# First adaLN scale of a two-layer decoder trunk: a quarter of three column groups computed on GpSimd

## The chip, the cores and the metric

One core of one Trainium2 chip runs the whole program. The metric is the device time of one execution in microseconds (us). The kernel before took 2666.12 us (median of 3 runs, 2662.95 to 2666.7).

## The reference, cut to what matters

Two decoder layers on 256 tokens of 2048 numbers, all in float32. The part that the change touches is the very first modulation of layer 0, before the first matrix product:

```python
cond = jax.nn.silu(c)                                   # c: 1 x 2048
mod = (cond @ ada_w[0] + ada_b[0])[:, None, :]          # ada_w[0]: 2048 x 12288
sh1, sc1, g1, sh2, sc2, g2 = jnp.split(mod, 6, axis=-1)
h = rmsnorm(x, norm_mix[0]) * (1.0 + sc1) + sh1         # sh1 the shift, sc1 the scale
y = nsa_mla_mixer(h, positions, rel_bias, even_w_in[0], ...)   # begins with h @ w_in
```

So `sc1` is a vector of 2048 numbers, each a sum over 2048 rows of `ada_w`, and `h @ w_in` can't begin on a piece of `h` before that piece of `sc1` and `sh1` is known.

## The kernel before, in words

**Prologue.** The first stage works in four column groups g = 0 to 3 of 512 columns. For each group SyncE (SP) loads four units of 512 rows x 512 columns (1 MB) of the scale's weights into the ring `RAW` (4 slots of 1 MB), four such units of the shift's weights into a ring of its own, `PRO`, and, in between, units of `even_w_in` for three column chunks c0, c1, c2 of the first projection into `RAW` as well. The order of the ring is fixed by `make_plan`: scale(g,0), c2's unit of group g-1, scale(g,1), scale(g,2), c0's unit g, c1's unit g, scale(g,3). SP waits in program order: before it loads unit s it waits until whoever reads unit s-4 has finished with that slot (`load` in `sync_program`).

**Scale, before.** `scale_rows(g, i)` on TensorE (PE) multiplies each 128-row piece of the unit by the matching column of `COND` (128 x 1): four float32 matmuls of 1 x 512, which the trace records as 8, collected in PSUM bank 6 over all 16 row pieces. ScalarE (ACT) copies the 1 x 512 row to `ROW` (`row_kept`, line 740). `columns(g)` turns it into columns: 4 matmuls with `ROW` as stationary operand and one element of ones (line 1279), and 4 with `ACC` (line 1283), where VectorE (DVE) has built the shift's partial products by `shift(g, i)` (lines 1832 and 1835).

**After `columns(g)`.** `opened(g)` on DVE (lines 1894, 1895, 1897) makes shift and gain, then for each of four row blocks DVE writes `TF` (line 1887), ACT writes the high part `AHI` (line 745), and DVE the low part `ALO` (line 1820). `opening_unit(c0, g)` on PE (lines 1199 to 1201) begins with the first of these `ALO` blocks; it is 24 matmuls of 128 x 512. On PE the order of a group is: `scale_rows(g,0)`, `opening_unit(c0, g-1)`, a bias piece (48 small matmuls, line 1238), `scale_rows(g,1)`, `opening_unit(c1, g-1)`, `scale_rows(g,2)`, a bias piece, `opening_unit(c2, g-1)`, `scale_rows(g,3)`, `columns(g)`. Thus `scale_rows(g,0)` stands between `columns(g-1)` and the opening unit that needs its result. After `columns(3)` no scale rows are left, and PE goes on to the last opening units with nothing in between.

**The other engines there.** For each weight unit ACT writes the high part `WHI` (line 622) and DVE the low part `WLO` (line 1722). GpSimd (POOL) does nothing in the prologue: it waits for `bias_kept`, to issue the load of a bias row (line 594).

After the prologue the same ring `RAW` feeds every product of the kernel, and PE works through all of them in order.

Of the kernel before, what the change touches and what calls it, by code (L numbers as in the profile page):

```python
# [20 lines left out]
ALU, ACT, AX = mybir.AluOpType, mybir.ActivationFunctionType, mybir.AxisListType  # L21

P, T, D, FF = 128, 256, 2048, 5632
KT = D // P
EPS, NEG = 1e-6, -1e30
RING = 4
SH1, SC1, G1, SH2, SC2, G2 = range(6)
# [3 lines left out]
ADA_ORDER = [((layer, seg), kt) for layer, seg, a, b in (  # L31
    (0, G1, 0, 16), (0, SC2, 0, 16), (0, SH2, 0, 16), (0, G2, 0, 16),
    (1, SH1, 0, 8), (1, SC1, 0, 16), (1, SH1, 8, 16), (1, SC2, 0, 16), (1, G1, 0, 16), (1, SH2, 0, 16), (1, G2, 0, 16))
    for kt in range(a, b)]
ADA_DONE = {vec: n + 1 for n, (vec, kt) in enumerate(ADA_ORDER) if kt == KT - 1}
ADA_APART = (1, SH1)
# [92 lines left out]
class Plan:  # L129

    def __init__(self):
        self.s = self.w = self.a = self.r = 0
        self.last = [None, None, None]
        self.kinds = []

    def unit(self, kind, **kw):
        u = Unit(kind, self.s, {"w": self.w, "a": self.a, "r": self.r}[kind], self.w, self.a, self.r, **kw)
        self.s += 1
        self.w += kind == "w"
        self.a += kind == "a"  # L140
        self.r += kind == "r"
        self.kinds.append(kind)
        return u

# [44 lines left out]
class Machine:  # L189

    def __init__(self, nc, t, ctx, known):
# [3 lines left out]
        def sb(name, shape, dt=F32):  # L195
            return ctx.enter_context(nc.sbuf_tensor(name, shape, dt))

        def overlay(*groups):

            size, made = 0, []  # L200
            for group in groups:
                with ExitStack() as one:
# [11 lines left out]
        ((self.AHI, self.ALO), (_, self.XG), (self.O, self.KN, self.RP, self.KRO, self.HCT, self.KCT, self.VCN), (_, self.BF)) = overlay(  # L214
            [("AHI", [P, KT, T], F32R), ("ALO", [P, KT, T], F32R)],
            [("XG_ROOM", [P, KT, T], F32), ("XG", [P, KT, T], F32)],
            [("O", [P, 16, T], F32), ("KN", [P, 8, T], F32), ("RP", [P, 2, 8, 64], F32), ("KRO", [P, 2, P], F32),
# [3 lines left out]
        (self.GHI, self.GLO), (self.PRO,), (self.XT, self.CQH, self.CQL), (_, self.QN), (self.KT_F, self.V_F) = overlay(  # L221
            [("GHI", [P, KT, T], F32R), ("GLO", [P, KT, T], F32R)],
            [("PRO", [P, RING, 2048], F32)],
# [17 lines left out]
        self.VC = sb("VC", [P, V_ALL])  # L241
        self.COND = sb("COND", [P, KT])
        self.GS = sb("GS", [P, 4, KT])
        self.SHM = sb("SHM", [P, 4, KT])
# [30 lines left out]
        self.W2C = self.S2[:, 1, :].rearrange("p (i k n) -> p i k n", i=2, k=2)  # L275
        self.RR = self.S2[:].rearrange("p a b -> p (a b)").rearrange("p (b h n) -> p b h n", b=2, h=8)
        self.PTC = (self.PT[:].rearrange("p a b c -> p (a b c)")[0:15, 0:1024], self.L[:].rearrange("p a b c -> p (a b c)")[0:15, 512:1536])
        self.OH = [s[:].rearrange("p a b -> p (a b)").bitcast(BF16)[:, 0:2048].rearrange("p (i t) -> p i t", t=P)
                   for s in (self.ST, self.S2)]

# [52 lines left out]
    def make_plan(self, t):  # L333
        plan = self.plan = Plan()
# [9 lines left out]
        opening = [[], [], []]  # L344

        def scale_unit(g, i):
            self.scales.append(plan.unit("r", vec=(0, SC1), kt=4 * i, kt0=512 * g))
            self.prologue += [self.scales[-1], ("shift", g, i)]

        def weight_unit(c, g):  # L350
# [26 lines left out]
        for n, count in enumerate((0, 2, 2, 2, 2, 1, 1, 3)):  # L377
            src, nk, cols, kt0 = rows(wout, 512 * (n % 2), 512)[n // 2]
# [31 lines left out]
        self.pair_in = {key: 12 + p for key, p in during.items()}  # L410
        self.ffns.append(ffn(1, (True, False, False), (none, none, none)))

        assert plan.a == len(ADA_ORDER) and plan.r == KT + 8

        self.pairs = [(n, h) for n in ("sel", "win", "mla") for h in (0, 2, 4, 6)] + [("fox", h) for h in range(0, 16, 2)]

# [59 lines left out]
def sync_program(block, nc, t, out, m):  # L476

    @block.sync
    def _(sp):
        kinds = m.plan.kinds  # L480

        def load(u):
            if u.s >= RING:

                if kinds[u.s - RING] == "r":
                    sp.wait_ge(m["row_used"].sem, u.r_before - sum(k == "r" for k in kinds[u.s - RING + 1:u.s]))
                elif kinds[u.s - RING] == "w":
                    sp.wait_ge(m["lo_ready"].sem, u.w_before - sum(k == "w" for k in kinds[u.s - RING + 1:u.s]))
                else:
                    sp.wait_ge(m["ada_used"].sem, u.a_before - sum(k == "a" for k in kinds[u.s - RING + 1:u.s]))  # L490
            slot, full = u.s % RING, m.raw_full[u.s % RING]
            if u.src is None:
                (layer, seg), kt = u.vec, u.kt
                if u.kind == "r":
                    at = D * seg + u.kt0
                    src = t["ada_w"][layer][P * kt:P * kt + 512, at:at + 512].rearrange("(k p) n -> p k n", p=P)
                    sp.dma_start(m.RAW[:, slot, :].rearrange("p (k n) -> p k n", n=512), src).then_inc(full, 16)
                    return
                sp.dma_start(m.RAW[:, slot, :], t["ada_w"][layer][P * kt:P * kt + P, D * seg:D * seg + D]).then_inc(full, 16)
                return  # L500
            dst = m.w_view(m.RAW, u).rearrange("p (k n) -> p k n", n=u.cols)
            if isinstance(u.src, tuple):
                sp.dma_start(dst[:, :, 0:24], u.src[0]).then_inc(full, 16)
                m[f"kr_full{slot}"].tick(sp.dma_start(dst[:, :, 24:88], u.src[1]), u.kt0, 16)
            else:
                sp.dma_start(dst, u.src).then_inc(full, 16)
# [78 lines left out]
def gpsimd_program(block, nc, t, out, m):  # L585

    @block.gpsimd
    def _(pool):
        rows = [t["ada_b"][layer:layer + 1, D * seg:D * seg + D] for layer, seg in ((0, G1), (0, G2), (1, G1), (1, G2))]
        last_use = [("bias_kept", 5), ("y_added", ("out0", 3)), ("y_added", ("down02", 3)), ("y_added", ("out1", 3))]  # L590
        for k, row in enumerate(rows):
            name, key = last_use[k]
            pool.wait_ge(m[name].sem, m[name].at(key))
            m["grow_bias"].tick(pool.dma_start(m.GROW[:], row.to_broadcast([P, D])), k, 16)
            pool.wait_ge(m["grow_bias"].sem, m["grow_bias"].at(k))
        pool.wait_ge(m["ada_sum"].sem, m["ada_sum"].at(((1, G2), 3)))
        m["gain_full"].tick(pool.dma_start(m.ACC[:], t["final_norm"].rearrange("(a n) -> a n", a=1).to_broadcast([P, D])), 0, 16)
        pool.wait_ge(m["gain_full"].sem, m["gain_full"].at(0))
# [434 lines left out]
def tensor_program(block, nc, t, out, m):  # L1033

    @block.tensor
    def _(pe):
        mm, turn = nc.tensor.matmul, nc.tensor.transpose

        def wait(name, key):
            pe.wait_ge(m[name].sem, m[name].at(key))  # L1040
# [219 lines left out]
        def scale_rows(g, i):  # L1260

            u = m.scales[4 * g + i]
            pe.wait_ge(m.raw_full[u.s % RING], 16 * (u.s // RING + 1))
            if g and i == 0:
                wait("row_kept", g - 1)
            for k in range(4):
                kt = u.kt + k
                ins = mm(m.PS[0:1, 6, :], m.COND[:, kt:kt + 1], m.RAW[:, u.s % RING, 512 * k:512 * k + 512], start=kt == 0, stop=kt == KT - 1)  # L1268
            m["row_used"].tick(ins, ("ada", u.n))
            if i == 3:  # L1270
                m["row_used"].noted["row", g] = m["row_used"].value

        def columns(g):

            wait("row_kept", g)
            if g:
                wait("bias_kept", 2 * g - 1)
            for j in range(4):
                mm(m.PS[:, 7, 4 * g + j:4 * g + j + 1], m.ROW[:, P * j:P * j + P], m.ONE[0:1, 0:1], start=True, stop=True)
            wait("shift_step", ("sum", g))  # L1280
            for j in range(4):
                at = 512 * g + P * j
                ins = mm(m.PS[:, 7, KT + 4 * g + j:KT + 4 * g + j + 1], m.ACC[:, at:at + P], m.ONE[:, 0:1], start=True, stop=True)
            m["columns"].tick(ins, g)
# [102 lines left out]
        for tb in range(2):  # L1387
            ins = turn(m.PS[:, 4, P * tb:P * tb + 88], m.GK[:, P * tb:P * tb + P], m.CON[0:88, C_ID:C_ID + 88])
# [65 lines left out]
        for i in range(2):  # L1454
            wait("st_copied", ("cmp", i))
            for j in range(2):
                ins = turn(m.PS[:, 6, 64 * i + 30 * j:64 * i + 30 * j + 30], m.ST[0:30, i, P * j:P * j + P], m.CON[0:30, C_ID:C_ID + 30])
# [6 lines left out]
        for g in range(2):  # L1464
            for k in range(2):
                ins = mm(m.PS[0:15, 5, P + P * g:P + P * g + P], m.HCT[:, 1, k, 15 * g:15 * g + 15], m.W2C[:, 1, k, :], start=k == 0, stop=k == 1)
        m["cmp_out"].tick(ins, 0)
        wait("vcn_ready", 0)
        for tb in range(2):
            for h in range(8):  # L1470
                at = 15 * (8 * tb + h)
                ins = mm(m.PS[:, 4, at:at + 15], m.XT[:, h, P * tb:P * tb + P], m.KCT[:, 15 * (h // 4):15 * (h // 4) + 15], start=True, stop=True)
# [30 lines left out]
        def out_unit(i, j):  # L1503
            c = m.even_out[i]
            unit(c, j, halves(m.GHI, m.GLO, c.w[j].kt0), ("lo_split", ("eo", 2 * j + 1)))
# [988 lines left out]
```

## Time and profile before

| | |
|---|---|
| median of 3 runs | 2666.12 us |
| profiled execution's own time | 2664.53 us |
| its span | 2662.7 us |
| PE busy | 2544.6 us (96%) |
| DVE busy | 1707.6 us (64%) |
| ACT busy | 1030.0 us (39%) |
| POOL busy | 3.0 us, 9 instructions |
| chain that ended last | PE 85%, DVE 8%, DMA 3% |
| scale rows (line 1268) | 128 records, 60.6 us busy, 2% of the chain |

The page has busy times and the chain of waits. The span is the stretch that the profile shows; the execution's own time is 1.8 us longer. A busy PE is not PE at its peak, since the ends of matmuls are modelled; the distance from one start to the next is the better measure. PEclk is the clock that TensorE was granted, as a share of full speed.

### The profile page before, as it was taken

What the parts mean: (1) busy time and instruction counts of PE and PEld (TensorE: products, weight loads), DVE (VectorE), ACT (ScalarE), POOL (GpSimd) and SP (SyncE); (2) the same over time, 40 slices, a digit from 0 to 9 for tenths busy, and PEclk for the clock granted to TensorE, in tenths of its full rate; (3) what the DMA queues carried; (4) which work ended last, traced back from release to release, by engine and by line L of the source; (5) the groups of instructions that cost most, each with busy time, mean ns of one, the idle gap of its engine ahead of it and who ended that gap; (6) DMA issues with size and microseconds to landing.
All of it is one profiled execution on the core that took longest, in us unless ns stands there. A gap on an engine that the chain in (4) does not pass through costs nothing.

```text
span 2662.7 us, 29253 instructions
## 1 busy us (share of the span) xinstructions
PE 2544.6 (96%) x11756; PEld 2036.4 (76%) x11756; DVE 1707.6 (64%) x1355; ACT 1030.0 (39%) x975; POOL 3.0 (0%) x9
## 2 busy tenths in 40 slices
PE   7999889889999999999989999999899999999998
PEld 3577577678877888888867888788688788888886
DVE  7768674767667666666656666668666654445445
ACT  2234343344333333333344444444433333333333
POOL 0000000000000000000000000000000000000000
PEclk9999888889999999999989999999999999999999
DMA  9879574757877687768769796898487755555553
GB/s 365 321 256 348 205 254 171 262 196 273 293 284 268 241 317 272 279 248 291 242 136 229 179 204 196 236 264 322 163 300 256 253 189 189 189 189 186 185 193 115
DMA packets 266196, 636.57 MB, mean 239 GB/s; under 512 B 15984, under 2 KB 26992, under 8 KB 244720
## 3 DMA queue, kind: packets, MB, share of 16 engines
q1 hardware_dynamic: 264800, 627.35, 70.9%
q0 software_dynamic: 720, 5.24, 0.5%
q10 hardware_dynamic: 576, 2.57, 0.2%
q8 instruction: 71, 1.16, 0.2%
q14 instruction: 29, 0.24, 0.0%
HBM read 633.03 MB, written 2.10 MB: 239 GB/s over the span
## 4 chain that ended last, share of the span: by engine, by line
PE 85%; DVE 8%; DMA 3%; ACT 2%; issue 2%; SPq 0%; DVEq 0%; ACTq 0%
PE PS L1048 24%; PE PS L1050 24%; PE PS L1049 24%; DVE WLO L1722 3%; PE PS L1268 2%; ACT WHI L622 1%; DVE ACC L1735 1%; PE PS L1328 1%; PE PS L1097 1%; PE PS L1199 1%; PE PS L1200 1%; PE PS L1201 1%; PE PS L1112 1%; PE PS L1348 1%; DMA RAW<-in_fox_w_in 1%
## 5 line engine op out<-in xcount | busy, mean ns | idle before, releaser
L1048 PE MATMUL PS<-WHI,AHI 128*128 128x512 f32 x2024 | 796.7, 394 | 20.8 <-DVE ALO L2256 8.9
L1050 PE MATMUL PS<-WHI,ALO 128*128 128x512 f32 x2024 | 789.1, 390 | 0.0
L1049 PE MATMUL PS<-WLO,AHI 128*128 128x512 f32 x2024 | 788.5, 390 | 0.0
L1722 DVE TENSOR_TENSOR WLO<-RAW,WHI 128x2048 fp32r<-128x2048 f32 (+2 forms) x222 | 503.7, 2269 | 362.0 <-ACT WHI L622 361.7
L622 ACT ACTIVATE WHI<-RAW 128x2048 fp32r<-128x2048 f32 (+2 forms) x222 | 421.3, 1898 | 741.2 <-PE PS L1050 576.9
L2300 DVE TENSOR_TENSOR WLO<-RAW,WHI 128x2048 fp32r<-128x2048 f32 x176 | 403.4, 2292 | 362.6 <-ACT WHI L927 361.7
L927 ACT ACTIVATE WHI<-RAW 128x2048 fp32r<-128x2048 f32 x176 | 337.4, 1917 | 591.9 <-PE PS L1050 558.7
L1048 PEld LDWEIGHTS PS<-WHI,AHI 128*128 128x128 f32 x2024 | 380.7, 188 | 105.9 <-issue 18.0
L1050 PEld LDWEIGHTS PS<-WHI,ALO 128*128 128x128 f32 x2024 | 380.3, 188 | 80.0
L1049 PEld LDWEIGHTS PS<-WLO,AHI 128*128 128x128 f32 x2024 | 380.8, 188 | 76.9 <-issue 0.2
L1048 PE MATMUL PS<-WHI,GHI 128*128 128x512 f32 x960 | 385.5, 402 | 22.9 <-DVE GLO L1820 13.6
L1050 PE MATMUL PS<-WHI,GLO 128*128 128x512 f32 x960 | 379.9, 396 | 0.0
L1049 PE MATMUL PS<-WLO,GHI 128*128 128x512 f32 x960 | 379.6, 395 | 0.0
L1048 PEld LDWEIGHTS PS<-WHI,GHI 128*128 128x128 f32 x960 | 184.4, 192 | 68.0 <-DVE GLO L1820 16.7
L1735 DVE SCALAR_TENSOR_TENSOR ACC<-RAW,COND,ACC 128x2048 f32<-128x2048 f32 x94 | 220.5, 2346 | 0.7
L1050 PEld LDWEIGHTS PS<-WHI,GLO 128*128 128x128 f32 x960 | 183.7, 191 | 39.7
L1049 PEld LDWEIGHTS PS<-WLO,GHI 128*128 128x128 f32 x960 | 184.2, 192 | 38.0 <-issue 0.5
L2311 DVE SCALAR_TENSOR_TENSOR ACC<-RAW,COND,ACC 128x2048 f32<-128x2048 f32 x60 | 140.7, 2346 | 0.1
L1268 PE MATMUL PS<-RAW,COND 128*1 128x512 f32 x128 | 60.6, 618 | 15.2 <-DMA RAW<-in_ada_w 15.2
L794 ACT ACTIVATE L<-L,NM 128x128 f32<-128x128 f32 x80 | 35.4, 444 | 72.6 <-DVE NM L2019 72.6
L1268 PEld LDWEIGHTS PS<-RAW,COND 128*1 128x1 f32 x128 | 9.7, 85 | 55.9 <-issue 51.0
L1835 DVE SCALAR_TENSOR_TENSOR ACC<-PRO,COND,ACC 128x512 f32<-128x512 f32 x60 | 45.0, 749 | 5.1 <-DMA PRO<-in_ada_w 3.4
(309 smaller groups left out, 1655.6 us busy)
## 6 DMA issues: line engine op xcount, KB each, us to landing
RAW<-in_ffn_w SPq DMA_DIRECT2D x264, 1024.0 KB, 5.1
RAW<-in_ada_w SPq DMA_DIRECT2D x176, 1024.0 KB, 5.9
RAW<-in_fox_w_in SPq DMA_DIRECT2D x64, 1024.0 KB, 8.2
RAW<-in_even_w_in SPq DMA_DIRECT2D x28, 1024.0 KB, 7.2
PRO<-in_ada_w SPq DMA_DIRECT2D x16, 1024.0 KB, 10.9
RAW<-in_even_w_out SPq DMA_DIRECT2D x16, 1024.0 KB, 6.3
RAW<-in_fox_w_out SPq DMA_DIRECT2D x16, 1024.0 KB, 5.9
GROW<-in_ada_b POOLq DMA_DIRECT2D x4, 1024.0 KB, 5.3
```

The lines of the kernel that those rows point to most:

```text
L622: A(m.w_view(m.WHI, u), m.w_view(m.RAW, u), ACT.Copy).then_inc(m["hi_ready"].sem, 1)
L794: m["exp_done"].tick(A(m.L[:, b, h, cols], m.L[:, b, h, cols], ACT.Exp, bias=m.NM[:, b, j:j + 1], accum_out=m.SM[:, b, j:j + 1]), p)
L927: A(m.WHI[:, (up.w0 + j) % 2, :], m.RAW[:, (up.s0 + s) % RING, :], ACT.Copy).then_inc(m["hi_ready"].sem, 1)
L1048: mm(dst(tb), xh, whi[:, k, :], start=first and k == 0, stop=False)
L1049: mm(dst(tb), xh, wlo[:, k, :], start=False, stop=False)
L1050: ins = mm(dst(tb), xl, whi[:, k, :], start=False, stop=last and k == nk - 1)
L1268: ins = mm(m.PS[0:1, 6, :], m.COND[:, kt:kt + 1], m.RAW[:, u.s % RING, 512 * k:512 * k + 512], start=kt == 0, stop=kt == KT - 1)
L1722: TT(m.w_view(m.WLO, u), m.w_view(m.RAW, u), m.w_view(m.WHI, u).bitcast(F32), ALU.subtract).then_inc(m["lo_ready"].sem, 1)
L1735: STT(out=acc[:], in0=raw, scalar=m.COND[:, kt:kt + 1], in1=acc[:], op0=ALU.mult, op1=ALU.add).then_inc(m["ada_used"].sem, 1)
L1835: ins = STT(out=acc, in0=src, scalar=by, in1=acc, op0=ALU.mult, op1=ALU.add)
L2300: TT(m.WLO[:, (up.w0 + j) % 2, :], m.RAW[:, (up.s0 + s) % RING, :], m.WHI[:, (up.w0 + j) % 2, :].bitcast(F32), ALU.subtract).then_inc(m["l ...
L2311: STT(out=m.ACC[:], in0=m.RAW[:, slot, :], scalar=m.COND[:, col], in1=m.ACC[:], op0=ALU.mult, op1=ALU.add).then_inc(m["ada_used"].sem, 1)
```

## The change

For g = 1, 2 and 3 the unit scale(g,0) gets the kind "g": PE skips it, and GpSimd multiplies its four 128 x 512 pieces by `COND`'s columns and adds them up in `SCALE[g % 2]` (4 tensor_scalar, 3 tensor_tensor, each waiting for the one before by a semaphore). The accumulation in bank 6 starts with scale(g,1), and so does the wait for the copy of the row before. `columns(g)` adds, for each of its four columns of scale, a second matmul with `SCALE` as stationary operand on all 128 partitions, into the same PSUM element; it now waits for the last GpSimd step. SP frees the ring slot of such a unit when all four pieces have been added. `SCALE` and the product's buffer `PART_G` lie in the room of `PT`, which is free in the prologue.

```diff
-            self.scales.append(plan.unit("r", vec=(0, SC1), kt=4 * i, kt0=512 * g))
+            self.scales.append(plan.unit("g" if g and i in POOL else "r", vec=(0, SC1), kt=4 * i, kt0=512 * g))
@@ sync_program, load
                 if kinds[u.s - RING] == "r":
                     sp.wait_ge(m["row_used"].sem, u.r_before - sum(k == "r" for k in kinds[u.s - RING + 1:u.s]))
+                elif kinds[u.s - RING] == "g":
+                    sp.wait_ge(m["scale_step"].sem, 4 * (u.g_before - sum(k == "g" for k in kinds[u.s - RING + 1:u.s])))
@@ gpsimd_program
+        def add_rows(g, i):
+            u = m.scales[4 * g + i]
+            pool.wait_ge(m.raw_full[u.s % RING], 16 * (u.s // RING + 1))
+            acc = m.SCALE[:, g % 2, :]
+            if g >= 3 and i == 0:
+                pool.wait_ge(m["columns"].sem, m["columns"].at(g - 2))
+            for k in range(4):
+                src, by = m.RAW[:, u.s % RING, 512 * k:512 * k + 512], m.COND[:, u.kt + k:u.kt + k + 1]
+                if i == k == 0:
+                    ins = nc.gpsimd.tensor_scalar(acc, src, by, None, ALU.mult)
+                else:
+                    pool.wait_ge(m["scale_step"].sem, m["scale_step"].value)
+                    m["scale_product"].tick(nc.gpsimd.tensor_scalar(m.PART_G, src, by, None, ALU.mult), (g, i, k))
+                    pool.wait_ge(m["scale_product"].sem, m["scale_product"].value)
+                    ins = nc.gpsimd.tensor_tensor(acc, acc, m.PART_G, ALU.add)
+                m["scale_step"].tick(ins, (g, i, k))
+
+        pool.wait_ge(m["silu_done"].sem, m["silu_done"].at("cond"))
+        for g in range(1, 4):
+            for i in POOL:
+                add_rows(g, i)
@@ tensor_program, scale_rows
+            if u.kind == "g":
+                return
             pe.wait_ge(m.raw_full[u.s % RING], 16 * (u.s // RING + 1))
-            if g and i == 0:
+            if g and i == len(POOL):
                 wait("row_kept", g - 1)
@@ tensor_program, columns
             if g:
+                wait("scale_step", (g, POOL[-1], 3))
                 wait("bias_kept", 2 * g - 1)
             for j in range(4):
-                mm(m.PS[:, 7, 4 * g + j:4 * g + j + 1], m.ROW[:, P * j:P * j + P], m.ONE[0:1, 0:1], start=True, stop=True)
+                mm(m.PS[:, 7, 4 * g + j:4 * g + j + 1], m.ROW[:, P * j:P * j + P], m.ONE[0:1, 0:1], start=True, stop=not g)
+                if g:
+                    mm(m.PS[:, 7, 4 * g + j:4 * g + j + 1], m.SCALE[:, g % 2, P * j:P * j + P], m.ONE[:, 0:1], start=False, stop=True)
```

On PE at the end of group 0, before the change, the scale rows of group 1 (line 1268, `PS<-RAW,COND`) stand between the column sums (1279, 1283) and the first opening unit (1199 to 1201):

```order
L1268 MATMUL PS<-RAW,COND 1x512 x8
L1253 MATMUL PS<-CON,X 128x128 x16
L1279 MATMUL PS<-CON,L 128x1 x4
L1283 MATMUL PS<-CON,ACC 128x1 x4
L1268 MATMUL PS<-RAW,COND 1x512 x4
L1199 MATMUL PS<-WHI,AHI 128x512
L1200 MATMUL PS<-WLO,AHI 128x512
```

The same place after the change (lines are some thirty higher; 1298 is scale rows, 1227 the opening unit):

```order
L1298 MATMUL PS<-RAW,COND 1x512 x8
L1281 MATMUL PS<-CON,X 128x128 x16
L1310 MATMUL PS<-CON,L 128x1 x4
L1316 MATMUL PS<-CON,ACC 128x1 x4
L1227 MATMUL PS<-WHI,AHI 128x512
L1228 MATMUL PS<-WLO,AHI 128x512
```

The opening unit now follows the column sums directly. On PE at the end of group 1, after the change (before it, the rows there read as in the first piece without the 16 turns; group 2 reads the same):

```order
L1298 MATMUL PS<-RAW,COND 1x512 x4
L1310 MATMUL PS<-CON,L 128x1
L1312 MATMUL PS<-CON,PT 128x1
L1310 MATMUL PS<-CON,L 128x1
L1312 MATMUL PS<-CON,PT 128x1
L1310 MATMUL PS<-CON,L 128x1
L1312 MATMUL PS<-CON,PT 128x1
L1310 MATMUL PS<-CON,L 128x1
L1312 MATMUL PS<-CON,PT 128x1
L1316 MATMUL PS<-CON,ACC 128x1 x4
L1227 MATMUL PS<-WHI,AHI 128x512
```

Four matmuls on `SCALE` (which lies in `PT`) have come in, and the scale rows behind the column sums are gone. On GpSimd, one unit of the three:

```order
L605 TENSOR_SCALAR PT<-RAW,COND 128x512 [waits raw_full2,silu_done]
L608 TENSOR_SCALAR PT<-RAW,COND 128x512 [waits scale_step]
L610 TENSOR_TENSOR PT<-PT 128x512 [waits scale_product]
L608 TENSOR_SCALAR PT<-RAW,COND 128x512 [waits scale_step]
L610 TENSOR_TENSOR PT<-PT 128x512 [waits scale_product]
L608 TENSOR_SCALAR PT<-RAW,COND 128x512 [waits scale_step]
L610 TENSOR_TENSOR PT<-PT 128x512 [waits scale_product]
```

These 7 instructions stand three times ahead of the load of the bias row, which was the first thing that GpSimd waited for. The order on DVE and ACT is as it was.

## Rows read from the trace of the kernel before

**Rows 1.** Windows of 20 us: busy time of each engine, clock, DMA share, GB/s.
```profile
core 0: us, PE busy (x) PEld busy (x) DVE busy (x) ACT busy (x) POOL busy (x), PEclk, DMA share, GB/s
40.00:60.00 20.00, 18.66 (x117) 11.02 (x117) 18.02 (x26) 3.99 (x5) 0.00 (x0) 1.00 0.97 353
...
160.00:180.00 20.00, 20.00 (x94) 16.63 (x93) 8.83 (x5) 9.14 (x6) 0.00 (x0) 1.00 0.50 178
...
200.00:220.00 20.00, 19.10 (x87) 15.48 (x86) 19.69 (x20) 8.21 (x8) 0.00 (x0) 1.00 0.96 353
```

**Rows 2.** PE in order of time, end of group 1: start, length, instruction, idle before.
```profile
77.38 1.05 PE L1279 MATMUL PS<-CON,L 1*128 1x1 f32 x8 [0.68 <-ACT L L740]
78.36 1.05 PE L1283 MATMUL PS<-CON,ACC 128*128 128x1 f32 x8
79.34 3.59 PE L1268 MATMUL PS<-RAW,COND 128*1 128x512 f32 x8
82.86 0.50 PE L1199 MATMUL PS<-WHI,AHI 128*128 128x512 f32 x1
```

**Rows 3.** PE in order of time, end of group 0.
```profile
37.88 1.97 PE L1253 MATMUL PS<-CON,X 128*128 128x128 f32 x16
...
41.74 3.59 PE L1268 MATMUL PS<-RAW,COND 128*1 128x512 f32 x8
46.68 0.47 PE L1199 MATMUL PS<-WHI,AHI 128*128 128x512 f32 x1 [1.34 <-DVE ALO L1820]
```

**Rows 4.** DVE in order of time, end of group 0.
```profile
42.33 2.28 DVE L1722 TENSOR_TENSOR WLO<-RAW,WHI 128x2048 fp32r<-128x2048 f32 x1
```

**Rows 5.** PE in order of time, end of group 3, where nothing stands between.
```profile
150.82 1.05 PE L1283 MATMUL PS<-CON,ACC 128*128 128x1 f32 x8
153.65 0.76 PE L1199 MATMUL PS<-WHI,AHI 128*128 128x512 f32 x1 [1.77 <-DVE ALO L1820]
```

**Rows 6.** The chain of waits there: start, length, what (half clock, then full).
```profile
158.25 0.43 PE PS L1200
...
159.71 0.23 PE PS L1201
```

**Rows 7.** Windows of 2 us on PE: busy, clock, DMA share, GB/s.
```profile
152.00:154.00 2.00, 0.35 (x1) 0.62 0.97 411
154.00:156.00 2.00, 2.00 (x6) 0.50 1.01 391
```

**Rows 8.** PE in order of time: scale rows after an earlier idle stretch.
```profile
26.96 4.88 PE L1268 MATMUL PS<-RAW,COND 128*1 128x512 f32 x8
```

**Rows 9.** DVE in order of time, end of group 1.
```profile
79.44 0.16 DVE L1894 TENSOR_TENSOR SHM<-PS,VC 128x4 f32<-128x4 f32 x1 [1.94 <-PE PS L1283]
...
82.60 0.48 DVE L1832 TENSOR_SCALAR ACC<-PRO,COND 128x512 f32<-128x512 f32 x1
83.12 2.33 DVE L1835 SCALAR_TENSOR_TENSOR ACC<-PRO,COND,ACC 128x512 f32<-128x512 f32 x3
```

**Rows 10.** SP's issues of scale(1,0), c0's unit 1, scale(2,0), c0's unit 2.
```profile
31.88 0.37 SPq L497 DMA_DIRECT2D RAW<-in_ada_w  x1
...
46.84 10.29 SPq L506 DMA_DIRECT2D RAW<-in_even_w_in  x2
...
66.35 0.37 SPq L497 DMA_DIRECT2D RAW<-in_ada_w  x1
...
82.96 10.40 SPq L506 DMA_DIRECT2D RAW<-in_even_w_in  x2
```

**Rows 11.** From issue to landing of the first three of these.
```profile
DMA to landing us min/median/max: 7.9/7.9/7.9
...
DMA to landing us min/median/max: 15.0/15.0/15.0
...
DMA to landing us min/median/max: 6.1/6.1/6.1
```

**Rows 12.** ACT in order of time: the high part of c0's unit 1.
```profile
62.90 1.91 ACT L622 ACTIVATE WHI<-RAW 128x2048 fp32r<-128x2048 f32 x1 [8.48 <-PE PS L1201]
```

More of the change, by code:

```diff
@@ L23 @@
 P, T, D, FF = 128, 256, 2048, 5632
+POOL = (0,)
 KT = D // P
@@ L131, in __init__ @@
     def __init__(self):
-        self.s = self.w = self.a = self.r = 0
+        self.s = self.w = self.a = self.r = self.g = 0
         self.last = [None, None, None]
@@ L136, in unit @@
     def unit(self, kind, **kw):
-        u = Unit(kind, self.s, {"w": self.w, "a": self.a, "r": self.r}[kind], self.w, self.a, self.r, **kw)
+        u = Unit(kind, self.s, {"w": self.w, "a": self.a, "r": self.r, "g": self.g}[kind], self.w, self.a, self.r, **kw)
         self.s += 1
@@ L141, in unit @@
         self.r += kind == "r"
+        u.g_before = self.g
+        self.g += kind == "g"
         self.kinds.append(kind)
@@ L277, in __init__ @@
         self.PTC = (self.PT[:].rearrange("p a b c -> p (a b c)")[0:15, 0:1024], self.L[:].rearrange("p a b c -> p (a b c)")[0:15, 512:1536])
+        self.SCALE = self.PT[:].rearrange("p a b c -> p (a b c)")[:, 0:1024].rearrange("p (i n) -> p i n", i=2)
+        self.PART_G = self.PT[:].rearrange("p a b c -> p (a b c)")[:, 1024:1536]
         self.OH = [s[:].rearrange("p a b -> p (a b)").bitcast(BF16)[:, 0:2048].rearrange("p (i t) -> p i t", t=P)
@@ L411, in make_plan @@
         self.ffns.append(ffn(1, (True, False, False), (none, none, none)))
-        assert plan.a == len(ADA_ORDER) and plan.r == KT + 8
+        assert plan.a == len(ADA_ORDER) and plan.r + plan.g == KT + 8
         self.pairs = [(n, h) for n in ("sel", "win", "mla") for h in (0, 2, 4, 6)] + [("fox", h) for h in range(0, 16, 2)]
@@ L493, in load @@
                 (layer, seg), kt = u.vec, u.kt
-                if u.kind == "r":
+                if u.kind in ("r", "g"):
                     at = D * seg + u.kt0
@@ L1267, in scale_rows @@
                 kt = u.kt + k
-                ins = mm(m.PS[0:1, 6, :], m.COND[:, kt:kt + 1], m.RAW[:, u.s % RING, 512 * k:512 * k + 512], start=kt == 0, stop=kt == KT - 1)
+                ins = mm(m.PS[0:1, 6, :], m.COND[:, kt:kt + 1], m.RAW[:, u.s % RING, 512 * k:512 * k + 512], start=i == (len(POOL) if g else 0) and k == 0, stop=kt == KT - 1)
             m["row_used"].tick(ins, ("ada", u.n))
```

## The prediction

> **What bounds the kernel now.** First the page: PE is busy 96% of the span and holds 85% of the chain, so I ask at each edit what PE's next start waits for. Then windows of 20 us [rows 1]: from 40 us on PE is near full, 18.66 of 20 us, while DVE has 18.02 and DMA a share of 0.97. At 160 to 180 us PE has 20.00 with DMA at 0.50: there the ring is what holds the loads back, and PE sets the pace. So what the prologue gains or loses on PE is carried on to the end; the DMA-full stretch at 200 us (share 0.96) begins from a ring that PE emptied, and shifts with it. Last, PE in order of time at the four places where `columns` ends [rows 2, 3, 5], since the change acts only there.
>
> **What is removed.** Three times `scale_rows(g,0)`. In group 2 it lasts from 79.34 to 82.86, 3.52 us [rows 2]; group 3 has the same. Three of them are 10.6 us, which is the most that the change could ever pay. It isn't what it pays, because these rows stand exactly where PE has to wait for DVE.
>
> *Place 1, columns(0) to c0's first unit.* Scale rows start at 41.74, and the opening unit at 46.68 after 1.34 us idle, released by DVE's `ALO` [rows 3]. DVE comes late because the split of c0 runs there from 42.33 for 2.28 us [rows 4]. Without the scale rows PE waits from 41.74 to the same 46.68. Gain: 0.
>
> *Places 2 and 3, columns(1) and columns(2).* There the scale rows hide the way from the column sums to the first `ALO`. Its length is seen at place 4, where nothing covers it: 1.77 us idle [rows 5]. So 3.52 - 1.77 = 1.75 us is gained at each, 3.5 us together.
>
> **What is added on PE.** Four matmuls with a 128 x 128 float32 stationary and one column, in each of columns(1), (2) and (3). The same kind is line 1283: four of them take from 78.36 to 79.34, 0.98 us [rows 2]. Nothing hides them, since the chain goes through the column sums: 3 x 0.98 = 2.9 us.
>
> **The clock.** At place 4 PE has waited 0.68 us for ACT's copy (as at [rows 2]), done two sets of one-column matmuls and stood idle for 1.77 us, and the granted clock falls: 0.62 and then 0.50 of full speed, that is 1.2 GHz in place of 2.4 [rows 7]. An opening matmul then takes 0.43 us to the next instead of 0.23 [rows 6]. From 153.65 [rows 5] to about 159.2 that is 13 matmuls, 13 x 0.20 = 2.6 us. At places 2 and 3 there was no such fall, with the same 0.68 us and columns of 2.0 us, because scale rows followed. After the change these two have what place 4 has, and 0.98 us more of one-column matmuls: I expect the fall at both. Place 1 gets an idle stretch of 4.94 us behind 3.9 us of turns and column sums (37.88 to 41.74) [rows 3]: a fall there too. Its price elsewhere: eight scale-row records take 4.88 us at the half clock [rows 8] against 3.59 [rows 3], 1.3 us. Between 1.3 and 2.6 I take the middle, 2.0 us a place: 3 x 2.0 = 6.0 us; the other bound is 0, if there is no fall. Place 4 pays its fall already, so nothing new there.
>
> **GpSimd.** Its elementwise work isn't in the trace before. The nearest rows are DVE's: 0.48 us for a 128x512 tensor_scalar, 2.33 / 3 = 0.78 us for a two-input one [rows 9]. Four and three of these are 4.3 us a unit as the lower end. As the upper end each instruction costs as much as DVE's 2048-wide one, 2.28 us [rows 4], or 16 us. I take 8 us, near the low end, as twice the nearest row. (The Trainium skill, GPSIMD Engine Reference, section 3.1, has one-input work at 769 ns for 512 elements and a two-input add of 2048 elements at 4497 ns; an estimate from that page is 4 x 0.77 + 3 x 1.12 = 6.4 us, and the sum would not change. No run here shows it yet.)
>
> Is that hidden? Scale(1,0) lands at 31.88 + 7.9 = 39.8 us [rows 10, 11] and its sum is first needed at columns(1), 77.4: 37 us. Scale(2,0) lands at 66.35 + 6.1 = 72.5 and is needed one group later. What can be late is the slot. SP waits for it to load c0's next unit, and behind it all later loads queue. Before, that issue came at 46.84 and 82.96; with 8 us it comes at 47.8 and 80.5, once 1 us later and once 2.5 us earlier. c0's unit 1 took 15.0 us to land behind a backlog, at 61.8 us, and ACT wants it at 62.90 [rows 11, 12]; at 353 GB/s [rows 1] a 1 MB load takes 3 us, so the issue may slip by some 10 us before it lands later at all. With 16 us it would issue at 55.8, still inside. Cost: 0, and only above 16 us does PE wait.
>
> **What GpSimd does to DVE.** It works at 39.8 to 48 us, through place 1's chain on DVE, and with 8 us or more just up to the end of columns at places 2 and 3 (72.5 + 8 = 80.5 against 80.3). At place 2 DVE had 1.94 us idle ahead of `SHM` [rows 9], and 0.98 us more now, as cover for a slip of its work before. No row before has the two engines side by side, so the bounds are 0 and 3 x 4.3 = 13 us, if DVE's chain stood still for all of GpSimd's work at its lowest price. I take 2 us: 1 at place 1, 0.5 at each of places 2 and 3, near 0 since most of it falls where DVE has slack.
>
> Here a rule speaks against the change. The Trainium skill's page SBUF — State Buffer, section "Who interferes with whom", says that a DVE instruction with two SBUF inputs and a GpSimd instruction that reads SBUF shut each other out for a whole instruction. Nothing before could show that. It stands behind the third rival below.
>
> **The sum.** -3.5 (places 2 and 3) + 2.9 (new column matmuls) + 6.0 (clock at places 1 to 3) + 2.0 (DVE slowed) = +7.4 us. On the profiled execution's own 2664.53 us (span 2662.7) that is 2671.9; its median stands 1.6 us higher at 2666.12, which gives 2673.5. I say 2673, +0.26%. A measurement of this kernel tells changes over 0.2%, 5.3 us, from none.
>
> **The rivals.**
> *No fall of the clock.* The same gain and matmuls, and PE stays at 2.4 GHz: -3.5 + 2.9 + 0 to 2 = -0.6 to +1.4 us, so 2666. For it: after columns(1) before, 2.7 us of waiting and one-column work cost no clock [rows 2]. Against it: place 4 fell with less idle than each place now has. This is the case on the other side, not slower: its place is the resume of PE behind columns(1) and (2), and it decides from the point where at least two of the three falls stay out (each is worth 2.0 us). Chance 0.22.
>
> *All of the scale rows are paid back.* PE's 10.6 us go and the waits behind them shrink, because `ALO` comes earlier: -10.6 + 2.9 = -7.7 us, 2658. Against it: the 1.34 us and 1.77 us of idle are released by DVE, after column sums that don't move [rows 3, 5]. Chance 0.04.
>
> *GpSimd and DVE shut each other out.* Each GpSimd instruction holds up the DVE chain at place 1 (split, gain, `TF`, `ALO`), and DVE's two-input work in turn stretches GpSimd's unit from 8 to 12 us or more, so that it runs into `opened` at places 2 and 3 too. With three blocks of 0.8 us at each of three places it is 7 us in place of 2: 2678 to 2680. For it: DVE is 18.02 of 20 us busy there [rows 1]. Chance 0.22, with the rule above as its reason.
>
> *GpSimd is so slow that the ring waits.* Above 16 us a unit the issue of c0's unit 1 comes late, and every load behind it; at 25 us, 9 us late in two of three groups with a backlog to eat: +8 to +15 us on top, 2685. Chance 0.07.
>
> My forecast, with the clock falling at all three places and little contention, has the remaining 0.45.
>
> **How the numbers follow.** The forecast's own range is +4 to +10 us: 2670 to 2676 on the median. The no-fall rival adds 2664 to 2667 below, contention adds up to 2680 and beyond. From 2664 to 2682 leaves out the paid-back case, most of the slow-ring case and edges of the others, under 2 in 10. Slower by over 5.3 us (above 2671.4): two thirds of the forecast, nearly all of contention and slow ring: 0.58. Faster by over 5.3: the paid-back case and a little more, 0.05. Within: 0.37.
>
> **What would show it.** In the profile after: at the end of columns(0) PE idles about 5 us, at columns(1) and (2) about 1.8 us, and granted clock of 0.5 follows at each of the three, with opening matmuls 0.43 us apart; columns takes 3.0 us in place of 2.0 in groups 1 to 3; the last opening matmul of the prologue ends some 7 us later and the difference stays constant to the end. GpSimd's unit is 6 to 12 us. SP's waits on GpSimd are short. If the clock column stays at 1.00 at places 1 to 3, the main term is wrong. If the opening units start late because of DVE instructions that wait between one another, the contention term is. If the difference at 160 us isn't that at the end, my claim that PE's shift is carried on fails.

## The result and the profile after

The changed kernel takes 2677.99 us (median of 10 runs, 2672.06 to 2690.71) against 2666.41 us (10 runs, 2662.6 to 2670.36): 1.0045 times as long, 95% interval 1.003 to 1.0061, or some 12 us slower. The profiled execution took 2690.71 us, the slowest of the ten, so it has to be taken apart before it is believed.

The page of the kernel after, first its span and part 1, then the clock row (TensorE's granted clock in 40 slices, in tenths):

```profile
span 2688.9 us, 29278 instructions
...
PE 2558.6 (95%) x11756; PEld 2054.5 (76%) x11756; DVE 1714.7 (64%) x1355; ACT 1029.9 (38%) x975; POOL 41.5 (2%) x30
...
PEclk9899898889999999999989999999899999999999
```

PE has lost 24 scale-row records and gained 24 column records, and is busy 14 us longer. Laid side by side by the number of matmuls still to come, the two traces differ by 12.3 us at 190 us and by 12.5 us still at 1040 us. The other 14 us of the span come later, in jumps, in code that the change doesn't touch. The first is behind a set of column sums at 1041 us, which in the kernel before reads (PE in order of time)

```profile
1041.24 3.63 PE L1097 MATMUL PS<-CON,ACC 128*128 128x1 f32 x32
```

and in the kernel after

```profile
1053.77 4.83 PE L1125 MATMUL PS<-CON,ACC 128*128 128x1 f32 x32
1058.46 0.78 PE L1076 MATMUL PS<-WHI,GHI 128*128 128x512 f32 x1
```

The same sums, slower, and a matmul at the half clock behind them: here the clock fell in one execution and not in the other. Two other kernels below (GpSimd beside a full PE, and the removal alone) show the same +3.2 us there, four others +1.6 us, the rest none. That part is scatter between executions. Of the 12 us of the prologue, 10.5 arise at the four places that the change touches; how much of these is scatter too is taken up under "The filling alone".

**Place 2, end of group 1** (answers to [rows 2]). PE in order of time: start, length, instruction, idle before.

```profile
80.77 0.38 PE L1310 MATMUL PS<-CON,L 1*128 1x1 f32 x2 [0.68 <-ACT L L768]
81.07 0.38 PE L1312 MATMUL PS<-CON,PT 128*128 128x1 f32 x2
...
82.93 0.43 PE L1312 MATMUL PS<-CON,PT 128*128 128x1 f32 x2
83.22 1.85 PE L1316 MATMUL PS<-CON,ACC 128*128 128x1 f32 x8
87.04 0.76 PE L1227 MATMUL PS<-WHI,AHI 128*128 128x512 f32 x1 [1.97 <-DVE ALO L1853]
```

The scale rows are gone and an idle stretch of 1.97 us stands there, as forecast. But the sums last from 80.77 to 85.07, 4.3 us, where they took 1.96 us before and I had 2.9. Two things are to be seen. The alternating kinds (a row on one partition, `SCALE` on 128) start every 0.31 us for two records, 0.155 each, where line 1283 had 0.122 [rows 2]. And the last eight take 1.85 us instead of 1.05. Windows of 2 us on PE show the clock there (busy, clock, DMA share, GB/s):

```profile
80.00:82.00 2.00, 1.32 (x9) 1.00 0.03 12
82.00:84.00 2.00, 2.00 (x13) 0.78 0.80 212
84.00:86.00 2.00, 1.07 (x6) 0.50 1.05 400
...
88.00:90.00 2.00, 2.00 (x6) 0.51 1.06 389
90.00:92.00 2.00, 2.00 (x10) 1.00 1.05 385
```

In this execution the clock falls in the sums, not in the idle stretch behind them. At places 3 and 4 it is the same: the sums take 4.9 and 4.5 us.

**Place 3.** DVE in order of time (answers to [rows 9]); the last line is place 4:

```profile
124.02 0.16 DVE L1927 TENSOR_TENSOR SHM<-PS,VC 128x4 f32<-128x4 f32 x1 [4.77 <-PE PS L1316]
...
124.48 2.05 DVE L1920 TENSOR_SCALAR TF<-XG,GS,SHM 128x256 f32<-128x256 f32 x2
...
164.51 0.73 DVE L1920 TENSOR_SCALAR TF<-XG,GS,SHM 128x256 f32<-128x256 f32 x2
```

GpSimd at that time:

```profile
113.22 1.81 POOL L605 TENSOR_SCALAR PT<-RAW,COND 128x512 f32<-128x512 f32 x1 [24.54 <-DMA RAW<-in_ada_w]
...
116.99 3.37 POOL L610 TENSOR_TENSOR PT<-PT 128x512 f32<-128x512 f32 x1
...
123.47 1.56 POOL L608 TENSOR_SCALAR PT<-RAW,COND 128x512 f32<-128x512 f32 x1
125.11 1.27 POOL L610 TENSOR_TENSOR PT<-PT 128x512 f32<-128x512 f32 x1
```

A split of DVE beside the third of these, and PE behind them:

```profile
116.95 2.29 DVE L1755 TENSOR_TENSOR WLO<-RAW,WHI 128x2048 fp32r<-128x2048 f32 x1 [0.38 <-ACT WHI L650]
...
127.01 0.77 PE L1227 MATMUL PS<-WHI,AHI 128*128 128x512 f32 x1 [3.03 <-DVE ALO L1853]
```

Two tensor_scalar of DVE take 2.05 us here; at place 4, where GpSimd is idle, the same two take 0.73. They end at 126.5, just behind GpSimd's instruction of 125.11 (it ends at 126.4). PE waits 3.03 us for the result, not 1.77. GpSimd's add of 116.99 in turn, beside a split of DVE, takes 3.37 us where others take 1.27. The rule that the prediction quotes is about DVE work with two SBUF inputs, so it bears on this split; a tensor_scalar with one such input falls under another point of the same section (the Trainium skill, SBUF — State Buffer, "Who interferes with whom"): a tensor_scalar that runs in one of DVE's 2-port modes can contend with GpSimd too. The trace agrees with both, with the 3.37 and the 2.05 us; in which mode DVE ran it doesn't show. A GpSimd unit takes 14.5, 12.4 and 13.2 us, not my 8.

The prologue from these traces, from the first column sum of a place to its opening unit, and that unit's 24 matmuls, in us before and after:

| place | sums to unit | unit |
|---|---|---|
| 1 | 6.9, 6.7 | 5.6, 7.6 |
| 2 | 5.5, 6.3 | 5.6, 6.9 |
| 3 | 5.5, 7.9 | 5.6, 7.4 |
| 4 | 3.8, 6.2 | half clock in both |

That is -0.2 + 0.8 + 2.4 + 2.4 = +5.4 us in the first column and +2.0 + 1.3 + 1.8 = +5.1 in the second. A further 1.6 us was lost ahead of place 1, where the clock fell at 35 us during scale rows of group 0, which the change leaves alone; 7 of the 10 kernels below show that too.

### The profile page after: what moved, and what is told of

It is laid out like the page before. It is cut to its first block, busy times and chain, and to the rows that moved or that the text cites. A ratio compares the mean times of both kernels' runs of the same rounds, so it can differ in the third digit from the quotient of the medians.

```text
span 2688.9 us, 29278 instructions
## 1 busy us (share of the span) xinstructions
PE 2558.6 (95%) x11756; PEld 2054.5 (76%) x11756; DVE 1714.7 (64%) x1355; ACT 1029.9 (38%) x975; POOL 41.5 (2%) x30
## 4 chain that ended last, share of the span: by engine, by line
PE 83%; DVE 8%; DMA 4%; ACT 3%; issue 2%; DVEq 0%; SPq 0%; ACTq 0%
PE PS L1076 23%; PE PS L1078 23%; PE PS L1077 23%; DVE WLO L1755 3%; PE PS L1298 2%; ACT WHI L650 2%; DMA RAW<-in_even_w_in 1%; PE PS L1361 1%; PE PS L1227 1%; PE PS L1125 1%; DVE ACC L1768 1%; PE PS L1228 1%; PE PS L1229 1%; DMA RAW<-in_ada_w 1%; DMA RAW<-in_fox_w_in 1%
## 5 line engine op out<-in xcount | busy, mean ns | idle before, releaser
L1076 PE MATMUL PS<-WHI,AHI 128*128 128x512 f32 x2024 | 799.3, 395 | 24.5 <-DVE ALO L2289 9.0
L1298 PE MATMUL PS<-RAW,COND 128*1 128x512 f32 x104 | 51.2, 640 | 16.6 <-DMA RAW<-in_ada_w 16.6
L1227 PE MATMUL PS<-WHI,AHI 128*128 128x512 f32 x96 | 42.0, 437 | 11.4 <-DVE ALO L1853 11.4
```

What stands on the lines that cost most here:

```text
L1076: mm(dst(tb), xh, whi[:, k, :], start=first and k == 0, stop=False)
L1227: mm(dst, xh, whi[:, k, :], start=kt == 0, stop=False)
```

## The experiments

Theory A: with the scale rows gone, PE stands open behind the column sums and pays the clock; the added matmuls are small. Theory B: GpSimd beside DVE costs. Theory C: the longer column sums themselves bring the clock down, gap or no gap. Each kernel below has one profiled execution, and the clock of one execution isn't that of all; the medians have 10 or 12. Each ratio is against runs of the kernel before on the same chip.

**Filler.** The changed kernel, with matmuls of the removed shape on other data put back at places 1 to 3.

```diff
             if u.kind == "g":
+                wait("row_kept", g - 1)
+                for k in range(4):
+                    mm(m.PS[0:1, 6, :], m.COND[:, k:k + 1], m.X[:, 0, 512 * k:512 * k + 512], start=k == 0, stop=k == 3)
                 return
```

> The changed kernel with four matmuls of the same shape as the removed scale rows (COND's column times a piece of X, result thrown away) put back on PE at the three places; GpSimd still does the work. Theory A (the gap behind the column sums and the lower clock after it cost the time): places 1 to 3 look as before the change again, the opening unit of group 0 runs at 1.00 of the clock, and what is left is the dearer column sums, 1.5 us each in groups 1 and 2 and 2.4 in group 3: +5 to +8 us against the kernel before. Rival B (GpSimd beside DVE is what costs): the filler changes nothing, +10 to +12 us. Rival C (the column sums alone let the clock fall): the filler itself runs at the half clock at places 2 and 3 and takes 4.9 us in place of 3.5, +8 to +10 us.

Measured: 2678.2 us, 1.0039 (1.0028 to 1.005), +10 us. PE in order of time at place 2:

```profile
82.36 1.84 PE L1319 MATMUL PS<-CON,ACC 128*128 128x1 f32 x8
84.14 5.62 PE L1294 MATMUL PS<-X,COND 128*1 128x512 f32 x8
89.69 0.50 PE L1227 MATMUL PS<-WHI,AHI 128*128 128x512 f32 x1
```

The gap is closed, the opening unit here runs at full clock, and nothing is won: the clock falls in the sums (1.84 us for eight), and the filler takes 5.6 us in place of 3.5. Place 3 reads the same. At place 1 the filler doesn't do what was expected of it. PE still waits for DVE, and the opening unit starts at the half clock (7.2 us in place of 5.6):

```profile
47.24 0.73 PE L1227 MATMUL PS<-WHI,AHI 128*128 128x512 f32 x1 [2.15 <-DVE ALO L1856]
```

Theory A alone is out, by the time and by place 2. C had both, though its cause, the length of the sums, is not shown by this (see "The filling alone").

**Removal alone.** No scale rows (g,0), nothing on GpSimd, sums as before; the kernel leaves out a quarter of the rows of three column groups. SP frees the slot of such a unit once it has landed.

```diff
-        pool.wait_ge(m["silu_done"].sem, m["silu_done"].at("cond"))
-        for g in range(1, 4):
-            for i in POOL:
-                add_rows(g, i)
@@ columns
-                wait("scale_step", (g, POOL[-1], 3))
-                if g:
-                    mm(... m.SCALE[:, g % 2, P * j:P * j + P] ...)
```

> Removal alone: PE leaves out scale rows (g,0) of groups 1 to 3, GpSimd does nothing, the column sums are as in the kernel before (so a quarter of the rows of three column groups is missing from the scale). Theory A: place 1 gains nothing and pays 2.0 us of clock; places 2 and 3 gain 1.75 us each and pay 1.3 to 2 us of clock if it falls: -1 to +3 us in all, although 10.6 us of PE work are gone. Rival (the idle behind the column sums costs nothing beyond its length, the clock stays): -3.5 us. Rival (PE's work counts in full): -10.6 us.

Measured: 2668.93 us, 1.0006 (0.999 to 1.0022), +1.6 us and not to be told from 0. At place 2:

```profile
80.88 1.05 PE L1309 MATMUL PS<-CON,ACC 128*128 128x1 f32 x8
83.70 0.77 PE L1223 MATMUL PS<-WHI,AHI 128*128 128x512 f32 x1 [1.77 <-DVE ALO L1846]
```

From the first sum (79.90) to the opening unit it is 3.80 us against 5.48: the gain of 1.7 us that I had, and the idle stretch of 1.77 us that place 4 had shown [rows 5]. The unit then pays it back at the half clock: 8.0 and 8.3 us at places 2 and 3, against 5.6. Here the fall comes in the idle stretch, where I had it. At place 1 it is 5.85 us from the first sum to the unit, as in the kernels below that keep these scale rows and leave GpSimd idle there (columns alone, in one block, the filling alone): no gain. 10.6 us of PE work bring nothing that can be measured: this half of the forecast is shown, to within the interval (-3 to +6 us). 10.6 us of gain is excluded.

**Columns alone.** The kernel before with only the four interleaved matmuls, on a cleared buffer.

```diff
+        m["cleared"].tick(nc.gpsimd.memset(m.SCALE, 0.0), 0)
@@ columns
-                mm(... m.ROW[:, P * j:P * j + P], m.ONE[0:1, 0:1], start=True, stop=True)
+                mm(... m.ROW[:, P * j:P * j + P], m.ONE[0:1, 0:1], start=True, stop=not g)
+                if g:
+                    mm(... m.SCALE[:, g % 2, P * j:P * j + P], m.ONE[:, 0:1], start=False, stop=True)
```

> The kernel before with only the four added column matmuls per group, interleaved as in the change, on a cleared buffer (they add zero). Theory A with the trace of the changed kernel: 16 interleaved records take 2.45 us there against 16 x 0.122 = 1.95 us, so 0.98 + 0.5 = 1.5 us a group, and the clock may fall inside them, which slows the rest of the sums and, at places 2 and 3, the scale rows behind: +4.5 to +8 us. Rival (the added matmuls cost 0.98 us each as the row of line 1283 has it, nothing else): +2.9 us.

Measured: 2676.98 us, 1.0028 (1.001 to 1.0046), +7.5 us. In its profile (2669.55 us, one of its fastest executions) place 2 has no fall of the clock and place 3 has one, so both prices stand side by side:

```profile
80.49 1.03 PE L1288 MATMUL PS<-CON,ACC 128*128 128x1 f32 x8
81.45 3.59 PE L1270 MATMUL PS<-RAW,COND 128*1 128x512 f32 x8
...
118.13 1.03 PE L1288 MATMUL PS<-CON,ACC 128*128 128x1 f32 x8
119.09 5.29 PE L1270 MATMUL PS<-RAW,COND 128*1 128x512 f32 x8
```

The sums begin at 78.07 and 115.72: 3.4 us each, +1.4 where I had +0.98. That is 4.2 us in three groups without any fall. At place 3 the scale rows behind them then take 5.29 us in place of 3.59 [rows 3]. By the medians this is the largest part of the loss.

**In one block.** The same four matmuls behind those of `ROW`, into columns of their own.

```diff
+            for j in range(4 if g else 0):
+                mm(m.PS[:, 6, j:j + 1], m.SCALE[:, g % 2, P * j:P * j + P], m.ONE[:, 0:1], start=True, stop=True)
```

> The kernel before with the same four added column matmuls a group as in the run with columns alone, but in one block behind those of ROW, into columns of their own in bank 6 (result not used), so the two kinds (1 and 128 partitions of stationary operand) don't alternate. Theory (alternating is what makes a record take 0.153 instead of 0.122 us): the sums last 2.95 us a group in place of 3.3, and the clock falls inside or behind them as often: +3 to +6 us against the kernel before, 1.3 us less than the alternating form. Rival (it is the full 128-partition load after a transposed row that is slow, or the clock alone): the same 3.3 us and more a group.

Measured: 2673.66 us, 1.0016 (1.0 to 1.0033), +4 us, at the edge of what can be told from 0. PE at place 2:

```profile
77.87 1.05 PE L1282 MATMUL PS<-CON,L 1*128 1x1 f32 x8 [0.68 <-ACT L L742]
78.85 1.05 PE L1284 MATMUL PS<-CON,PT 128*128 128x1 f32 x8
79.76 1.03 PE L1288 MATMUL PS<-CON,ACC 128*128 128x1 f32 x8
80.72 5.29 PE L1270 MATMUL PS<-RAW,COND 128*1 128x512 f32 x8
```

The sums take 2.85 us: in a block the matmuls cost 0.9 us, close to the 0.98 of the row I had used, and the other form adds 0.5. The edit changes two things, though. The matmuls no longer alternate, and they no longer add into the element that the one before has just written. Which of the two costs the 0.5 us no run tells. The intervals of the two ratios overlap, so only the trace shows this difference.

**GpSimd alone.** PE does all as before, GpSimd beside it does the same units for nothing.

```diff
-            self.scales.append(plan.unit("g" if g and i in POOL else "r", ...))
+            self.scales.append(plan.unit("r", ...))
@@ sync_program, load
+                for n, side in enumerate(m.side):
+                    if side.s == u.s - RING:
+                        sp.wait_ge(m["scale_step"].sem, 4 * (n + 1))
```

> The kernel before with GpSimd doing its multiply-adds on the same three units beside PE, which does all the scale rows as before; SP frees a slot when both are done; GpSimd's result is not used. Theory A: DVE's chain at place 1 is 0.8 us longer, at places 2 and 3 the delay (0.2 and 1.25 us) is hidden under 3.5 us of scale rows: 0 to +2 us. Rival B (GpSimd and DVE shutting each other out is the main cost, 2.2 us and more through slower splits and loads): +4 us or more.

Measured: 2668.69 us, 0.9997 (0.9984 to 1.001): no difference, within 4 us. DVE's chain at place 3 shows that this isn't for lack of contention:

```profile
117.57 1.89 DVE L1919 TENSOR_SCALAR TF<-XG,GS,SHM 128x256 f32<-128x256 f32 x2
```

1.89 us again in place of 0.73, hidden under scale rows that last until 122.2. Place 1 isn't covered to the end, and there the interference shows:

```profile
48.11 0.47 PE L1231 MATMUL PS<-WHI,AHI 128*128 128x512 f32 x1 [1.10 <-DVE ALO L1852]
```

PE idles 1.10 us, against 0.3 in the kernels without GpSimd whose sums come at the same time: 0.8 us, as expected. Where PE is covered, GpSimd's work and its interference are free.

**Sums joined in the row.** The changed kernel, `SCALE` added in bank 6 by one 1 x 512 matmul, column sums as before.

```diff
+            if g and i == 3:
+                wait("scale_step", (g, POOL[-1], 3))
+                ins = mm(m.PS[0:1, 6, :], m.ONE[:, 0:1], m.SCALE[:, g % 2, :], start=False, stop=True)
```

> The changed kernel, but GpSimd's partial sums join the row in bank 6 by one matmul of 1 x 512 (ones as stationary, SCALE moving) at the end of scale_rows(g,3), and the column sums are those of the kernel before. Theory A' (after the first four experiments: the added and interleaved column matmuls are about two thirds of the loss, by their own length and by the clock that falls inside them; the open gap costs the rest): the removal alone measured +0 to +2 us, the added matmul is two records of 0.44 us, 0.88 a group or 2.6 in all: +2 to +5 us. Rival (GpSimd's work costs when the gap is open): +7 us or more. Rival (the gap, not the columns, is the loss): +10 us.

Measured: 2673.75 us, 1.0026 (1.0015 to 1.0037), +7 us by the ratio: between the theory's upper end and the rival. At place 2:

```profile
82.67 1.05 PE L1316 MATMUL PS<-CON,ACC 128*128 128x1 f32 x8
86.65 0.77 PE L1227 MATMUL PS<-WHI,AHI 128*128 128x512 f32 x1 [2.93 <-DVE ALO L1853]
```

The wait is 2.93 us where the removal alone had 1.77: 1.2 us of GpSimd's interference, laid open by the gap, and the same at place 3. So it costs with the gap and not without it. The sums take 2.0 us again in place of 4.3, for one added matmul of 0.9 us ahead of them. By the ratios this form loses less than the changed kernel, but the intervals overlap.

**Another unit.** scale(g,2) on GpSimd in place of scale(g,0), so that the rows behind the sums stay on PE.

```diff
-POOL = (0,)
+POOL = (2,)
```

> The changed kernel with scale(g,2) on GpSimd in place of scale(g,0), column sums as in the change. PE keeps the scale rows that stand behind the column sums, and loses ones that stand between dense products. Theory A': 10.6 us saved in full, the dearer column sums cost the 7.5 us of the run with columns alone: -1 to -5 us against the kernel before. Rival (GpSimd's unit of 12 to 14 us now holds the ring slot too long or delays DVE's splits): the saving is lost, 0 or above.

Measured: 2666.6 us, 0.9995 (0.9983 to 1.0008), -1 us. By the medians 11 us better than the change with unit 0, but no gain against the kernel before that can be told from 0. In its profile PE waits 0.72 and 1.22 us inside the sums of places 2 and 3, for DVE's shift sums.

**Another unit, joined in the row.** Both edits.

> Both: scale(g,2) on GpSimd and the partial sums joined in bank 6 by one matmul a group. Theory A': 3 x (3.52 - 0.88) = -7.9 us, no clock falls at places 2 and 3, place 1 as before: -6 to -9 us against the kernel before. Rival (GpSimd holds slot or DVE): between -4 and +2.

Measured: 2662.92 us, 0.9985 (0.9973 to 0.9997), -4 us: faster than the kernel before, by less than the 7.9 us of PE work, and in the range of the rival. The interval overlaps that of the run above. PE in order of time at place 2:

```profile
75.37 1.05 PE L1312 MATMUL PS<-CON,L 1*128 1x1 f32 x8 [0.68 <-ACT L L768]
78.20 1.10 PE L1316 MATMUL PS<-CON,ACC 128*128 128x1 f32 x8 [1.79 <-DVE ACC L1868]
79.24 5.19 PE L1298 MATMUL PS<-RAW,COND 128*1 128x512 f32 x8
```

and DVE ahead of it:

```profile
64.88 4.76 DVE L1868 SCALAR_TENSOR_TENSOR ACC<-PRO,COND,ACC 128x512 f32<-128x512 f32 x4
```

The four cost 1.19 us each beside GpSimd, 0.78 without [rows 9]. DVE is now the later of the two, PE waits 1.79 us inside the sums (2.38 at place 3), and the scale rows behind run at the half clock (5.19 us). These two waits, 4.2 us, are what DVE takes back of the saving. That the pause is what brings the clock down is not shown: the filling alone, below, has the fall without it.

**And place 4 filled.** c2's unit 2 behind columns(3), in this kernel (on ACT and DVE the splits of c1's unit 3 move behind `opened(3)`):

```diff
+                if g < 3:
+                    opening_unit(c2, g - 1)
@@
             columns(g)
+        opening_unit(c2, 2)
```

> The kernel of e7, and in group 3 c2's opening unit 2 (24 matmuls, 5.5 us) is moved behind columns(3), where PE stood idle for 1.77 us and then paid 2.6 us of clock; ACT's and DVE's splits of c1's unit 3 are moved behind opened(3) so that nothing waits in a ring. Theory: a further -4.4 us, so -11 to -13 us against the kernel before. Rival (the later split of c1's unit 3 makes PE wait, or the loads behind it come late): -5 to -8 us, with an idle stretch ahead of c1's unit 3.

Measured: 2663.39 us, 0.9985 (0.9974 to 0.9996): no better. PE at place 4:

```profile
139.70 3.59 PE L1300 MATMUL PS<-RAW,COND 128*1 128x512 f32 x8 [1.42 <-DMA RAW<-in_ada_w]
...
147.62 1.87 PE L1318 MATMUL PS<-CON,ACC 128*128 128x1 f32 x8 [1.75 <-DVE ACC L1872]
149.35 0.77 PE L1229 MATMUL PS<-WHI,AHI 128*128 128x512 f32 x1
```

The idle behind the sums is gone and has come back inside them, again for DVE's shift sums. And the last scale rows, from in front of which c2's unit was taken, wait 1.42 us for their load. Neither form of my expectation had these places.

**The filling alone**, the same three moves in the kernel before, without GpSimd:

```diff
             columns(g)
+        opening_unit(c2, 2)
```

> The kernel before, nothing on GpSimd, with only c2's opening unit 2 moved behind columns(3) and the splits of c1's unit 3 behind opened(3). Theory: PE no longer idles 1.77 us at place 4 and no clock falls there: -4.4 us against the kernel before, -3 to -5. Rival (the wait moves to the sums: with c2's unit gone ahead of them, columns(3) comes 5.4 us earlier and waits for DVE's shift sums, as in the combined version): -1 to -2 us. Rival (the later split of c1's unit 3 delays the loads behind it): 0 or above.

Measured: 2665.56 us against 2669.59, 0.9986 (0.9969 to 1.0002), -4 us, the expected size but not clear of 0. PE goes from the sums straight on at 151.83 and the low clock ends early, after six matmuls in place of thirteen. The first four lines are places 2 and 3:

```profile
78.83 1.19 PE L1285 MATMUL PS<-CON,ACC 128*128 128x1 f32 x8
79.94 5.10 PE L1270 MATMUL PS<-RAW,COND 128*1 128x512 f32 x8
...
116.66 1.46 PE L1285 MATMUL PS<-CON,ACC 128*128 128x1 f32 x8
118.04 6.53 PE L1270 MATMUL PS<-RAW,COND 128*1 128x512 f32 x8
...
150.65 1.32 PE L1285 MATMUL PS<-CON,ACC 128*128 128x1 f32 x8
151.83 0.78 PE L1201 MATMUL PS<-WHI,AHI 128*128 128x512 f32 x1
...
154.54 0.47 PE L1201 MATMUL PS<-WHI,AHI 128*128 128x512 f32 x1
```

Places 2 and 3 are the more telling part of this trace, because up to there the code is that of the kernel before. The sums are the short ones, nothing pauses inside or behind them, and yet the clock falls in the sums at both places: from the first sum to the opening unit it takes 7.1 and 8.8 us, where the trace of the kernel before has 5.5 and 5.5. So 5 us of difference at these two places can arise between two executions of like code. Counted over places 2 and 3 of the profiles in which scale rows or the filler follow the sums and PE waits for nothing but ACT's copy: with the old sums (the kernel before, GpSimd alone, the filling alone) the clock fell in 3 of 6, with longer ones (the filler, columns alone, in one block) in 5 of 6. With the gap open (the change, the removal alone, sums joined in the row) it fell in 6 of 6. The direction is that of theories A and C, but these are few executions.

## Why the prediction was right, and where its sizes were off

**Places of the gain: right.** Place 1 gains nothing, and places 2 and 3 gain 1.7 us each of the 3.5 that were removed there, as the removal alone shows.

**The added column matmuls: the term that was mis-sized.** I had 0.98 us a group, 2.9 in all, "the same kind is line 1283". The sums grew by 2.3, 2.9 and 2.5 us, 7.7 in all. Of each, 0.9 is the four matmuls, 0.5 the interleaving with those of the row (3.4 against 2.85 us in the two forms), together 4.2 in the three groups, and the other 3.5 us are the clock falling inside the sums, which I had put only behind them. With columns alone the kernel loses 7.5 us (2.7 to 12), where I had 2.9.

**The clock: right in kind, its price in part luck.** I had 2.0 us for each of three opening units and they lost 2.0, 1.3 and 1.8, so 5.1 for my 6.0. But I tied the fall to the idle stretch. The filler closed that stretch and the loss stayed. I also took it from one profile that the kernel before has no fall at places 2 and 3, "because scale rows followed". That step is wrong: with scale rows behind the same sums the clock fell at place 3 beside GpSimd and at both places in the filling alone. So part of this is paid before the change too, in some executions, and how much of the 5.1 us is new stays open.

**GpSimd.** My 8 us a unit were 13.4 on average, outside the 6 to 12 that I had named as a sign, but below the 16 us from which I had it cost, and the ring did not make PE wait. Contention: I took 2.0 us; DVE's way from `SHM` to the opening unit grew by 0.8, 0.2 and 1.2 us, 2.2 in all. At place 1 the table doesn't show it, since the sums came 1.6 us later there and DVE's split did not, so that DVE's chain started sooner behind them. It was not the main cost: alone, beside a full PE, no cost could be measured.

**The sum.** 7.4 us were forecast, 11.6 measured (8 to 16 by the interval). That is slower, as said, and inside 2664 to 2682, but above the 4 to 10 us that I gave my own mechanism; by size the rival of contention, with 2678 to 2680, was nearer, for a reason that the runs don't bear out. In terms of my sum the profile has -3.4 (gain), +7.7 (sums), +5.1 (clock in the opening units) and +1.1 (contention and rest), 10.5 us for my -3.5 + 2.9 + 6.0 + 2.0. The term that was mis-sized is that of the column matmuls. By the experiments' medians: removal +1.6, columns +7.5, GpSimd 0 are 9; each of these is known to 4 or 5 us, so what is left of the 12 can't be told from nothing. The open contention of 0.2 and 1.2 us at places 2 and 3 is seen in the trace.

**The shift carried on to the end: not shown.** In the traces of before and after it held from 190 to 1040 us, within half a microsecond. But in six of the other ten traces the difference to the kernel before shrinks or turns by 2.8 to 5.5 us between 190 and 900 us, mostly in like matmuls that run at the half clock in one execution and not in the other. That this one pair of profiles agrees so well is luck.

## What to carry to other kernels

Work that stands in front of a wait is cover, and moving it away pays only what exceeds the wait. Take instead the same work from between dense products: together with the join in the row this turned +12 us into -4 here. A partial result is joined more cheaply by one wide matmul (0.9 us) than by four one-column ones interleaved with the others on the chain (1.4 us and more); in one block these took 0.9 us as well, so it is the form that must be looked at. The traces show this, the medians only suggest it. An engine that seems to have slack (DVE here) must be looked at again once the bound engine is made shorter. And one profile doesn't say where the clock falls: two traces of like code differed by 5 us at two places.

## What was not expected of the hardware

- One-column float32 matmuls whose stationary operand alternates between 1 and 128 partitions, each pair adding into one element, started 0.155 us apart; in blocks of one kind 0.122.
- Behind 0.68 us of idle and some 1 to 3 us of one-column matmuls the granted clock fell to 0.50 inside these matmuls in several executions, although PE counts as 2.00 of 2.00 us busy there (82 to 84 us of the change: clock 0.78, then 0.50). Eight such records then take 1.85 us in place of 1.05. In other executions of like code it didn't fall.
- GpSimd's 128x512 tensor_scalar took 1.56 us at the shortest, DVE's 0.48; its tensor_tensor 1.26 to 3.37 us, the longest beside DVE's splits.
